# Layer 1's last modulation third moved into layer 0's choice, the sorts started before their vectors, and SP's loads reordered

## The chip, the cores and the metric
The kernel runs on one core of a Trainium2 chip. The metric is the device time of one execution in microseconds. A core has TensorE (PE, matrix products), VectorE (DVE), ScalarE (ACT), GpSimd (POOL) and SyncE (SP), which here only issues DMAs. Before the change the median of three runs was 3538.36 us (3538.24 to 3542.34).

## The reference
Two transformer layers work on 1024 tokens and 256 context tokens of width 1024, all in float32. Each layer has a modulation, a mixer (attention in layer 0; attention and a scan in layer 1) and a mixture of 16 experts.
```
def ada_modulation(cond, w_mod, b_mod):
    mod = jax.nn.silu(cond) @ w_mod + b_mod
    return jnp.split(mod[..., None, :], 6, axis=-1)      # sh1, sc1, gt1, sh2, sc2, gt2

def expert_choice_ffn(h, w_router, w_gate, w_up, w_down):
    aff = jax.nn.softmax(jnp.einsum('bnd,de->bne', h, w_router), axis=-1)
    gate, idx = lax.top_k(jnp.swapaxes(aff, 1, 2), cap)
    xg = h[bidx, idx]
    hid = jax.nn.silu(jnp.einsum('becd,edf->becf', xg, w_gate)) * jnp.einsum('becd,edf->becf', xg, w_up)
    out = jnp.einsum('becf,efd->becd', hid, w_down) * gate[..., None]
    return jnp.zeros_like(h).at[bidx, idx].add(out)
```
Layer 0 uses differential attention, a = p0 - lam * p1 of two softmax maps (the subtracted maps). Each expert takes its 128 best tokens (layer 0 also 32 context tokens).

## The kernel before
The kernel is one program of stages in order: modulation (first third), projection, differential attention, local attention, output mix with routing, experts of layer 0, then the front, scan, attention, mix and experts of layer 1. A stage has one written program for each engine, and semaphores between them. Weights are loaded by SP in the written order of its queue. Objects named "...Ahead" hold tiles of a following stage, and are loaded by the stage before it.

**Modulation.** The two 1024 x 6144 matrices are cut in six thirds of 2048 columns. `first` is multiplied in its own stage, `rest[0]` to `rest[4]` in the gaps of other stages by `RestOfModulation`. A third is eight steps: step n loads 128 rows (1 MB) into one of the slots, and `multiply` (matmuls at L312) makes four products of 128 x 2 by 128 x 512, in four strips of partitions of one PSUM bank. `add_bias` (L320) adds the bias in four VectorE instructions, `store` (L326) writes the third to DRAM. In the attention three thirds were done (`rest[0]`, `rest[1]` of layer 0 and `rest[4]`, the last of layer 1): 24 steps in pairs, after every second item, for items 0 to 23 of 40 (four heads of ten query tiles). The weights (`attn_a_mod_w`) are loaded from ACT's queue.

**The attention.** For each item TensorE makes scores (L1014) and turned weights (L1026), and multiplies the values (L1039). VectorE takes the scores out of PSUM (L939) and subtracts the maps (L960). GpSimd rotates the next head's queries and keys (L717 to L722) and normalises the output of a former head (L841 to L845).

**The choice.** `Choice.select` on VectorE sorts: 16 rounds of MAX8 (L2197), FIND_INDEX8 (L2198) and MATCH_REPLACE8 (L2200), each waiting for the one before, over the affinities of all experts. TensorE turns the result (L2235), VectorE makes indices, and GpSimd gathers the rows of expert 0 (`experts_xg` L2437, in layer 0 also `experts_xc` of the context, L2439). TensorE transposes them (L2639, L2642); VectorE and ACT scale them by `gain` and `shift` into `experts_xT`. Ahead of the sort VectorE waited for those vectors and made `gain` (L2569). In layer 0 TensorE meanwhile made the eight `opening` steps (`rest[2]`), whose first four weights the stage before had put in the tile of the down weights (`down_ahead_wd`), with PSUM bank `Y[1]`; and the four additions came after the first transposes. After the last expert comes `closing` (`rest[3]`).

**The experts.** For each expert TensorE makes 16 groups of eight products with the gate and up weights (L2684), the transposes of the next expert, and the products with the down weights (L2650, L2659). VectorE and ACT take the two halves of the result out of `Y[1]` and `Y[0]` (counters `yv` and `ya`), GpSimd adds the rows into DRAM. SP loads gate and up weights in two halves of 2 x 2 MB when TensorE has freed each, then 2 x 2 MB of down weights. Its order was: vectors, opening steps, gates and ups of expert 0, the store of the opening third with a wait, a wait for the first transposes, down weights of expert 0, `following.load` (layer 0: `FrontAhead`, 25 DMAs with two loads of 2 MB of `front_ahead_w`; layer 1: `FinishAhead`, ten DMAs), then the loop from expert 1 on.

## Time and profile before
| what | value |
|---|---|
| median of 3 runs | 3538.36 us (3538.24 to 3542.34) |
| the profiled execution's own time | 3540.56 us |
| its span | 3538.8 us |
| PE busy | 3262.9 us (92%) |
| DVE busy | 1251.9 us (35%) |
| ACT busy | 973.0 us (27%) |
| POOL busy | 494.0 us (14%) |
| HBM over the span | 192 GB/s |

The span runs from the first to the last record of the profiled execution. Times in rows are microseconds from its start. A line of a timeline is: start, duration, engine (PEld is the weight load of TensorE, "q" behind a name the engine's queue of instructions), line of the kernel, operation, output<-inputs, sizes, count, and in brackets how long the engine stood idle before it and what it waited for. One product of 32-bit numbers has two records. A line of the windows is: stretch, its length, busy time with count of PE, PEld, DVE, ACT and POOL, the granted TensorE clock as a share of full speed, the mean busy share of the DMA engines, and GB/s. A line of the DMA issues ends with the median time from issue to landing. L numbers are lines of the kernel before.

### The profile page before, as it was taken

What the parts mean: (1) busy time and instruction counts of PE and PEld (TensorE: products, weight loads), DVE (VectorE), ACT (ScalarE), POOL (GpSimd) and SP (SyncE); (2) the same over time, 40 slices, a digit from 0 to 9 for tenths busy, and PEclk for the clock granted to TensorE, in tenths of its full rate; (3) what the DMA queues carried; (4) which work ended last, traced back from release to release, by engine and by line L of the source; (5) the groups of instructions that cost most, each with busy time, mean ns of one, the idle gap of its engine ahead of it and who ended that gap; (6) DMA issues with size and microseconds to landing.
All of it is one profiled execution on the core that took longest, in us unless ns stands there. A gap on an engine that the chain in (4) does not pass through costs nothing. (4 is left out here: it accounts for less than half of the span.)

```text
span 3538.8 us, 53560 instructions
## 1 busy us (share of the span) xinstructions
PE 3262.9 (92%) x20520; PEld 2456.0 (69%) x20520; DVE 1251.9 (35%) x3001; ACT 973.0 (27%) x2247; POOL 494.0 (14%) x650
## 2 busy tenths in 40 slices
PE   6999989889993999999999989899799299999998
PEld 4888756667541878878778655566674188888886
DVE  3312178767655011011000153566675500101013
ACT  3211156756441011111110152235554111111111
POOL 0000234210010011111101130244101000000002
PEclk8999999989995999999999999999999699999999
DMA  6336454062355977777777640100314498888887
GB/s 222 125 104 113 117 193 166 15 159 80 117 200 183 332 248 268 256 246 263 257 253 265 218 170 0 54 21 30 99 38 161 142 365 317 316 316 313 313 313 267
DMA packets 377129, 675.77 MB, mean 191 GB/s; under 512 B 76232, under 2 KB 115016, under 8 KB 370752
## 3 DMA queue, kind: packets, MB, share of 16 engines
q1 hardware_dynamic: 343152, 561.60, 45.9%
q0 software_dynamic: 13616, 47.32, 5.5%
q10 hardware_dynamic: 20208, 64.87, 4.9%
q8 instruction: 88, 1.44, 0.2%
q14 instruction: 65, 0.53, 0.0%
HBM read 587.75 MB, written 92.20 MB: 192 GB/s over the span
## 5 line engine op out<-in xcount | busy, mean ns | idle before, releaser
L2684 PE MATMUL experts_gu_ps<-experts_xT,experts_wg 128*128 128x160 f32 (+1 forms) x4096 | 554.6, 289 | 12.7 <-DMA experts_wu<-in_l_w_up 7.0
L2684 PEld LDWEIGHTS experts_gu_ps<-experts_xT,experts_wg 128*128 128x128 f32 x4096 | 531.3, 193 | 28.0 <-issue 26.7
L2684 PE MATMUL experts_gu_ps<-experts_xT,experts_wu 128*128 128x160 f32 (+1 forms) x4096 | 550.1, 287 | 0.0
L2684 PEld LDWEIGHTS experts_gu_ps<-experts_xT,experts_wu 128*128 128x128 f32 x4096 | 525.7, 192 | 0.0
L2581 DVE TENSOR_TENSOR experts_hid<-experts_sil,experts_gu_ps 128x160 f32<-128x160 f32 (+1 forms) x256 | 77.8, 304 | 931.3 <-ACT experts_sil L2518 931.3
L2518 ACT ACTIVATE experts_sil<-experts_gu_ps 128x160 f32<-128x160 f32 (+1 forms) x256 | 74.3, 290 | 1110.8 <-PE experts_gu_ps L2684 1110.8
L2650 PE MATMUL experts_y_ps<-down_ahead_wd,experts_hid 128*128 128x512 f32 x512 | 228.3, 599 | 0.0
L2650 PE MATMUL experts_y_ps<-experts_wd,experts_hid 128*128 128x512 f32 x512 | 224.0, 595 | 1.2 <-DVE experts_hid L2581 1.2
L2650 PEld LDWEIGHTS experts_y_ps<-experts_wd,experts_hid 128*128 128x128 f32 x512 | 96.0, 190 | 118.1 <-issue 114.8
L2599 DVE TENSOR_SCALAR experts_y<-experts_y_ps,experts_wt 128x512 f32<-128x512 f32 x31 | 23.3, 750 | 436.9 <-PE experts_y_ps L2650 436.9
L2650 PEld LDWEIGHTS experts_y_ps<-down_ahead_wd,experts_hid 128*128 128x128 f32 x512 | 94.6, 190 | 114.4 <-issue 113.7
L2964 PE MATMUL front_pb_ps<-kept_hT,front_ahead_w 128*128 128x512 f32 (+1 forms) x384 | 138.7, 521 | 0.7 <-DVE kept_dt L3015 0.7
L2463 POOL DMA_INDIRECT moe<-experts_y,experts_ixs x31 | 49.4, 1594 | 575.4 <-DVE experts_y L2599 575.4
L3420 PE MATMUL scan_f_ps<-scan_w,kept_hT 128*128 128x512 f32 x256 | 117.1, 600 | 0.0
L2964 PEld LDWEIGHTS front_pb_ps<-kept_hT,front_ahead_w 128*128 128x128 f32 x384 | 72.4, 190 | 62.7 <-issue 59.4
L594 PE MATMUL proj_x_ps<-proj_ahead_w,proj_hT 128*128 128x256 f32 x480 | 115.1, 383 | 0.0
L594 PEld LDWEIGHTS proj_x_ps<-proj_ahead_w,proj_hT 128*128 128x128 f32 x480 | 92.0, 192 | 12.6
L2458 POOL DMA_INDIRECT moe<-experts_yc,experts_ixsc x16 | 25.7, 1609 | 530.7 <-ACT experts_yc L2535 530.7
L877 ACT ACTIVATE attn_a_e<-attn_a_e,attn_a_nmx 128x1280 f32<-128x1280 f32 (+1 forms) x80 | 96.6, 1209 | 9.9 <-DVE attn_a_e L939 9.9
L2504 ACT ACTIVATE experts_xT<-experts_tp_ps,experts_shift,experts_gain 128x128 f32<-128x128 f32 x132 | 49.6, 456 | 134.9 <-PE experts_tc_ps L2642 75.4
L1039 PE MATMUL attn_a_o_ps<-attn_a_v,attn_a_aT 128*128 128x128 f32 x672 | 83.1, 277 | 3.9 <-ACT attn_a_sq L892 3.9
L1039 PEld LDWEIGHTS attn_a_o_ps<-attn_a_v,attn_a_aT 128*128 128x128 f32 x672 | 78.3, 192 | 11.2 <-issue 7.5
(490 smaller groups left out, 4991.4 us busy)
## 6 DMA issues: line engine op xcount, KB each, us to landing
experts_wg<-in_l_w_gate SPq DMA_DIRECT2D x64, 2048.0 KB, 8.2
experts_wu<-in_l_w_up SPq DMA_DIRECT2D x64, 2048.0 KB, 13.1
down_ahead_wd<-in_l_w_down SPq DMA_DIRECT2D x32, 2048.0 KB, 14.9
experts_wd<-in_l_w_down SPq DMA_DIRECT2D x32, 2048.0 KB, 11.7
attn_a_mod_w<-in_l_w_mod ACTq DMA_DIRECT2D x20, 1024.0 KB, 6.4
proj<-proj_ob ACTq DMA_DIRECT2D x60, 256.0 KB, 2.3
proj_ahead_w<-in_l_w_in SPq DMA_DIRECT2D x6, 2048.0 KB, 9.5
mix_xr<-res SPq DMA_DIRECT2D x18, 512.0 KB, 3.6
```

The lines of the kernel that those rows point to most:

```text
L594: mm = nc.tensor.matmul(to[:, left], by[k], at[k], start=(k == 0 and n in (0, 1, 5)), stop=(k == HALF - 1 and n in (3, 5, 6)), skip_group_ ...
L877: nc.scalar.activation(e[:, s, m, 0:w], e[:, s, m, 0:w], ACT.Exp, bias=nmx[:, s, m:m + 1], scale=-1.0, accum_out=sums[:, s, m:m + 1]).then ...
L1039: mm = nc.tensor.matmul(O[:, 0:P], aT[:, kt, :], v[:, h % 2, kt, :], start=(kt * P == keys(t)[0]), stop=(kt == last))
L2458: pool.indirect_dma_start(moe.rearrange("t (j c) -> (t j) c", j=4), bass.IndirectOffsetOnAxis(ap=ixsc[:, 0:1], axis=0), yc[:], None, compu ...
L2463: pool.indirect_dma_start(moe, bass.IndirectOffsetOnAxis(ap=ixs[:, 0:1], axis=0), y[:], None, compute_op=ALU.add).then_inc(s_done, 16)
L2504: a = nc.scalar.activation(xT[:, k, 0:CAPX], TP[1][:, k - 4, :], ACT.Identity, bias=shift[:, 0, k:k + 1], scale=gain[:, 0, k:k + 1])
L2518: nc.scalar.activation(sil[:, f % 2, :], GU[f % 2][:, 0, 0:N], ACT.Silu).then_inc(sil_done, 1)
L2581: nc.vector.tensor_tensor(hid[:, f, :], sil[:, f % 2, :], GU[f % 2][:, 1, 0:N], ALU.mult).then_inc(hid_done, 1)
L2650: mm = nc.tensor.matmul(Y[h][:], hid[:, k, 0:CAPX], wd[:, h, k, :], start=(k == 0), stop=(k == KD - 1))
L2684: mm = nc.tensor.matmul(GU[f % 2][:, part, 0:N], w[:, h, k, c * P:(c + 1) * P], xT[:, k, :], start=(k == 0), stop=(k == KD - 1))
L2964: mm = nc.tensor.matmul(pb[n % 4][:, 0:width], w[:, s, k, at:at + P], hT[:, k, first:first + width], start=(k == 0), stop=(k == KD - 1))
L3420: mm = nc.tensor.matmul(F[:], kept.hT[:, k, t * P:(t + 1) * P], w[:, int(kind == "q"), k, :], start=(k == 0), stop=(k == KD - 1))
```

## The change
- `RestOfModulation` takes a list of PSUM banks `accs`, and third a uses bank a modulo their number. `store_third` stores one third and waits until it has landed.
- The attention multiplies two thirds (16 steps). The opening of layer 0's choice multiplies two, `rest[2]` and `rest[4]`, in `Y[1]` and `Y[0]`: 16 steps over the same four slots. The first third's additions are made inside the sort, after its eleventh round; the second's after the transposes. `ya` is counted up by one as `yv` is.
- In both layers the sort stands ahead of the wait for the vectors and of `gain`.
- SP's order: in layer 1 `following.load` comes ahead of the wait for the transposes; in layer 0 the two loads of `front_ahead_w` become `load_columns` and come after the gates and ups of expert 1 and the store of the second third.
```diff
+    def store_third(self, sp, a):
+        for j in range(GROUPS):
+            sp.wait_ge(self.added, START + GROUPS * a + j + 1)
+            sp.dma_start(self.rest[a][2][:, j * BANK:(j + 1) * BANK], self.rows[strip(j), a, :]).then_inc(self.stored, 16)
+        sp.wait_ge(self.stored, START + 16 * GROUPS * (a + 1))
...
-            opening = RestOfModulation(nc, st, K, [down.third], Y[1], "opening", down.places, down.w_in)
+            opening = RestOfModulation(nc, st, K, down.thirds, [Y[1], Y[0]], "opening", down.places, down.w_in)
...
                 link(nc.vector.match_replace(work[:], val[:, j:j + 8], work[:], -1.0))
+            if between and j == 80:
+                between()
...
                 load_gates_up(0)
                 if down:
+                    opening.store_third(sp, 0)
+                if ends:
+                    following.load(sp)
+                sp.wait_ge(tp_done, START + 1)
+                if down:
                     sp.wait_ge(opening.multiplied, START + opening.steps)
-                    opening.store(sp)
-                sp.wait_ge(tp_done, START + 1)
                 load_down(0)
-                following.load(sp)
-                with sp.Fori(0, E - 1) as e:
+                if not ends:
+                    following.load(sp)
+                load_gates_up(1)
+                if not ends:
+                    opening.store_third(sp, 1)
+                    following.load_columns(sp)
+                load_down(1)
+                with sp.Fori(1, E - 1) as e:
                     load_gates_up(e + 1)
                     load_down(e + 1)
...
                 choice.begin(dve, link)
+                choice.select(dve, link, first_third if down else None)
                 dve.wait_ge(vec_in, START + 16 * (2 * conds + 1))
                 for c in range(conds):
                     nc.vector.scalar_tensor_tensor(gain[:, c, :], gain[:, c, :], 1.0, g[:], ALU.add, ALU.mult).then_inc(vec_done, 1)
                 dve.wait_ge(vec_done, START + conds)
-                choice.select(dve, link)
                 transposed(0)
                 if down:
                     for j in range(GROUPS):
-                        opening.add_bias(dve, 0, j)
-                    dve.wait_ge(opening.added, START + GROUPS)
+                        opening.add_bias(dve, 1, j)
+                    dve.wait_ge(opening.added, START + GROUPS * 2)
                     dve.sem_inc(yv, 1)
+                    dve.sem_inc(ya, 1)
...
-                    pe.wait_ge((ya, yv)[h], START + e + (0, mods)[h])
+                    pe.wait_ge((ya, yv)[h], START + e + mods)
...
-                    differential_attention(nc, K, attn_ahead, near_ahead, projs[n], n, mixed, rest[:2] + rest[4:])
+                    differential_attention(nc, K, attn_ahead, near_ahead, projs[n], n, mixed, rest[:2])
...
-                down = over.enter_context(DownAhead(nc, K, rest[2])) if with_ctx else None
+                down = over.enter_context(DownAhead(nc, K, [rest[2], rest[4]])) if with_ctx else None
```

## Rows read from the trace of the kernel before
**Rows 1.** The page: the span of the profiled execution.
```profile
span 3538.8 us, 53560 instructions
```
**Rows 2.** Windows: head 2 of the attention (with four pairs), then head 3 (with none).
```profile
568.46:633.93 65.47, 62.56 (x441) 40.25 (x441) 55.93 (x141) 43.69 (x103) 28.28 (x17) 1.00 0.37 127
633.93:692.83 58.90, 55.51 (x376) 38.93 (x377) 48.03 (x134) 43.57 (x103) 13.78 (x10) 1.00 0.06 17
```
**Rows 3.** Timeline of TensorE, attention: start us, us, instructions, idle before and its releaser.
```profile
576.25 1.90 PE L312 MATMUL attn_a_m_ps<-attn_a_mod_w,cond_gate 128*2 128x512 f32 x16
578.08 0.70 PE L1014 MATMUL attn_a_s_ps<-attn_a_ahead_kT,attn_a_ahead_qT 64*128 64x256 f32 x4
...
588.56 0.70 PE L1014 MATMUL attn_a_s_ps<-attn_a_ahead_kT,attn_a_ahead_qT 64*128 64x256 f32 x4 [0.81 <-DVE attn_a_e L939]
```
**Rows 4.** Timeline of VectorE, the same stretch.
```profile
578.83 0.48 DVE L939 TENSOR_SCALAR_CACHE_REDUCE attn_a_e<-attn_a_s_ps,attn_a_nmx 128x256 f32<-128x256 f32 x1 [3.27 <-PE attn_a_s_ps L1014]
...
619.48 0.48 DVE L939 TENSOR_SCALAR_CACHE_REDUCE attn_a_e<-attn_a_s_ps,attn_a_nmx 128x256 f32<-128x256 f32 x1 [2.49 <-PE attn_a_s_ps L1014]
```
**Rows 5.** Timeline of the choice of layer 0, VectorE and TensorE.
```profile
1085.72 0.41 DVE L2192 MEMSET experts_strip<- 32x1 f32 x4 [0.34 <-PEq L1712]
1091.93 0.24 DVE L2569 SCALAR_TENSOR_TENSOR experts_gain<-experts_gain,experts_g 128x8 f32<-128x8 f32 x2 [5.80 <-DMA experts_g<-in_l_g_pre_ffn]
1092.21 0.69 DVE L2197 MAX8 experts_val<-listed_work 80x8 f32<-80x512 f32 x1
...
1095.19 1.04 PE L312 MATMUL experts_y_ps<-down_ahead_wd,cond_gate 128*2 128x512 f32 x8 [3.59 <-DMA down_ahead_wd<-in_l_w_mod]
...
1102.79 1.89 PE L312 MATMUL experts_y_ps<-down_ahead_wd,cond_gate 128*2 128x512 f32 x8 [0.63 <-DMA down_ahead_wd<-in_l_w_mod]
...
1129.64 0.40 PE L2235 MATMUL experts_tp_ps<-ident,experts_val 80*128 80x80 f32 x1 [24.96 <-DVEq L2208]
...
1138.86 1.94 PE L2639 MATMUL experts_tp_ps<-ident,experts_xg 128*128 128x128 f32 x8 [8.42 <-DMA experts_xc<-normed,experts_ixgc]
...
1143.89 2.83 DVE L320 TENSOR_TENSOR experts_opening_rows<-experts_y_ps,experts_opening_bias 2x512 f32<-2x512 f32 x4
```
**Rows 6.** Tile attn_a_mod_w: landing times of 24 step weights (1 MB each).
```profile
DMA to landing us min/median/max: 4.8/6.5/11.0
```
**Rows 7.** DMA issues of 1138:1146 (queues near empty), then of 1206:1216 (queues full).
```profile
experts_xc<-normed,experts_ixgc POOLq DMA_INDIRECT x1, 3.7
...
experts_xc<-normed,experts_ixgc POOLq DMA_INDIRECT x1, 6.6
```
**Rows 8.** Timeline of SP's queue from the choice of layer 0 to expert 1.
```profile
1148.09 1.02 SPq L2382 DMA_DIRECT2D down_ahead_wd<-in_l_w_down  x2
...
1180.91 1.38 SPq L2279 DMA_DIRECT2D front_ahead_w<-in_l_w_in  x2
```
**Rows 9.** Windows: TensorE clock and DMA, layer 0 (choice, then the start of expert 1).
```profile
1120.00:1124.00 4.00, 0.00 (x0) 0.00 (x0) 3.83 (x10) 0.00 (x0) 0.00 (x0) 0.50 0.92 340
...
1207.40:1212.00 4.60, 4.60 (x17) 4.60 (x18) 0.00 (x0) 0.00 (x0) 0.55 (x3) 0.50 1.04 308
```
**Rows 10.** Timeline of TensorE: the start of expert 1 of layer 0.
```profile
1207.36 4.61 PE L2684 MATMUL experts_gu_ps<-experts_xT,experts_wg 128*128 128x160 f32 x16 [7.04 <-DMA experts_wu<-in_l_w_up]
1214.44 2.34 PE L2684 MATMUL experts_gu_ps<-experts_xT,experts_wg 128*128 128x160 f32 x16
1216.62 2.34 PE L2684 MATMUL experts_gu_ps<-experts_xT,experts_wu 128*128 128x160 f32 x16
```
**Rows 11.** Timeline and one window of the choice of layer 1.
```profile
2776.53 0.37 SPq L2385 DMA_DIRECT2D experts_shift<-mod  x1
2780.33 0.69 DVE L2197 MAX8 experts_val<-listed_work 48x8 f32<-48x512 f32 x1
...
2802.00:2816.00 14.00, 0.00 (x0) 0.00 (x0) 13.38 (x31) 0.00 (x0) 0.00 (x0) 0.50 0.00 1
...
2820.15 1.12 POOL L2437 DMA_INDIRECT experts_xg<-normed,experts_ixg  x1 [0.88 <-DVEq L2229]
```

More of the change, by code:

```diff
@@ L281, with __init__ @@
     SLOTS = 4
-    def __init__(self, nc, st, K, rest, acc, name="mod", places=None, w_in=None):
-        self.nc, self.rest, self.acc, self.gate = nc, rest, acc, K.gate
+    def __init__(self, nc, st, K, rest, accs, name="mod", places=None, w_in=None):
+        self.nc, self.rest, self.accs, self.gate = nc, rest, accs, K.gate
         self.steps = KD * len(rest)
@@ L308, in multiply @@
         pe.wait_ge(self.w_in[n % self.slots], START + 16 * (n // self.slots + 1))
-        if k == 0 and a >= 1:
-            pe.wait_ge(self.added, START + GROUPS * a)
+        acc = self.accs[a % len(self.accs)]
+        if k == 0 and a >= len(self.accs):
+            pe.wait_ge(self.added, START + GROUPS * (a - len(self.accs) + 1))
         for j in range(GROUPS):
-            mm = self.nc.tensor.matmul(self.acc[strip(j), :], self.gate[:, :, k], self.places[n % self.slots][:, j * BANK:(j + 1) * BANK],
+            mm = self.nc.tensor.matmul(acc[strip(j), :], self.gate[:, :, k], self.places[n % self.slots][:, j * BANK:(j + 1) * BANK],
                                        start=(k == 0), stop=(k == KD - 1))
@@ L319, in add_bias, with __init__ @@
             dve.wait_ge(self.bias_in, START + 16 * GROUPS * len(self.rest))
-        self.nc.vector.tensor_tensor(self.rows[strip(j), a, :], self.acc[strip(j), :], self.bias[strip(j), a, :], ALU.add).then_inc(self.added, 1)
+        self.nc.vector.tensor_tensor(self.rows[strip(j), a, :], self.accs[a % len(self.accs)][strip(j), :], self.bias[strip(j), a, :], ALU.add).then_inc(self.added, 1)
+    def store_third(self, sp, a):
[3 more added lines that the diff above has]
+        sp.wait_ge(self.stored, START + 16 * GROUPS * (a + 1))
     def store(self, sp):
         for a in range(len(self.rest)):
-            for j in range(GROUPS):
-                sp.wait_ge(self.added, START + GROUPS * a + j + 1)
-                sp.dma_start(self.rest[a][2][:, j * BANK:(j + 1) * BANK], self.rows[strip(j), a, :]).then_inc(self.stored, 16)
-        sp.wait_ge(self.stored, START + 16 * GROUPS * len(self.rest))
+            self.store_third(sp, a)
 class DownAhead(Ahead):
-    def __init__(self, nc, K, third):
+    def __init__(self, nc, K, thirds):
         super().__init__(nc, K, "down_ahead")
-        self.third = third
+        self.thirds = thirds
         self.wd = self.sb("wd", [P, 2, KD, BANK])
@@ L341, in load @@
         for n, place in enumerate(self.places):
-            eng.dma_start(place, self.third[0][n * P:(n + 1) * P, :]).then_inc(self.w_in[n], 16)
+            eng.dma_start(place, self.thirds[0][0][n * P:(n + 1) * P, :]).then_inc(self.w_in[n], 16)
 def row(vec, width):
@@ L792, in differential_attention @@
         M = st.ps("m", [P, BANK])
-        later = RestOfModulation(nc, st, K, rest, M)
+        later = RestOfModulation(nc, st, K, rest, [M])
         rows = first.rows
@@ L2192, in begin, with select @@
             link(self.nc.vector.memset(self.strip[j * CAPC:(j + 1) * CAPC, :], float(j)))
-    def select(self, dve, link):
+    def select(self, dve, link, between=None):
         nc, work, val, idx, idf = self.nc, self.work, self.val, self.idx, self.idf
@@ L2277, in load, with load_columns @@
         sp.dma_start(self.cw[:, TAPS, :], columns(self.conv_b)).then_inc(self.cw_in, 16)
+    def load_columns(self, sp):
         for s in range(2):
@@ L2333, in experts @@
             gates_up = [w[:, h].rearrange("p k n -> p (k n)")[:, s * THIRD:(s + 1) * THIRD] for h in range(2) for w in (wg, wu) for s in range(2)]
[L2334 to L2335 removed]
+            opening = RestOfModulation(nc, st, K, down.thirds, [Y[1], Y[0]], "opening", down.places, down.w_in)
+            closing = RestOfModulation(nc, st, K, [last_third], [GU[0][:].rearrange("p a b -> p (a b)")], "closing", gates_up)
         if with_ctx:
@@ L2460, in scatter @@
                     pool.wait_ge(yv, START + e + mods + 1)
-                    pool.wait_ge(ya, START + e + 1)
+                    pool.wait_ge(ya, START + e + mods + 1)
                     pool.sem_inc(begun, 1)
@@ L2566, in _, with first_third @@
                 choice.begin(dve, link)
+                def first_third():
+                    for j in range(GROUPS):
+                        opening.add_bias(dve, 0, j)
+                choice.select(dve, link, first_third if down else None)
                 dve.wait_ge(vec_in, START + 16 * (2 * conds + 1))
```

1 line of the change is left out of this document (removed).

## The prediction
> **What bounds the kernel now.** I read the page first (span 3538.8 us [rows 1]; TensorE busy nearly throughout, so only places where TensorE waits or does avoidable work can pay), then the windows of the attention, then the timelines of the three stretches that the diff touches: the heads of layer 0's attention, the two choices (the sort of the affinities before the experts), and the start of the experts' loop. TensorE's own multiplications of the experts are not changed. So the whole effect must come out of these:
> - In the attention TensorE is nearly full: a head with four pairs of modulation steps takes 65.47 us with 62.56 us of TensorE, the next one without pairs 58.90 us with 55.51 us [rows 2].
> - In both choices VectorE's sort alone is the path. In layer 0 it starts at 1092.21, after a wait of 5.80 us for the small vectors; VectorE was free from 1086.13 (1085.72 + 0.41) [rows 5]. TensorE waits 24.96 us for the sort's end, and then 8.42 us for the gathered rows [rows 5]. In layer 1 the sort starts at 2780.33, and the stage at 2776.53 [rows 11].
> - At the start of expert 1 of layer 0 TensorE stands 7.04 us for the weights, and the first two groups after that run slowly [rows 10].
>
> **The attention: eight steps go.** The last third of layer 1's modulation was multiplied here in steps 16 to 23, as four pairs. A pair takes TensorE 1.83 us (576.25 to 578.08) [rows 3], four 7.3 us. Head 2 holds just these four and head 3 none: 65.47 - 58.90 = 6.57 us between them, 7.05 us in TensorE's busy time [rows 2]. Not all of it comes back, since VectorE is the other limit in head 2: it is busy 55.93 us there against 48.03 us [rows 2], for its operation with two operands in SBUF is slower beside GpSimd's rotations. After the first and the last pair VectorE waited 3.27 and 2.49 us for scores [rows 4], so these two pairs are worth their full 1.83. After the second pair TensorE already waited 0.81 us for VectorE [rows 3], so that pair only moves the wait and gives nothing; the third I count at 1.4. With a little for the four additions (2.83 us of VectorE as in [rows 5]) that go, the sum is 1.83 + 0 + 1.4 + 1.83 + 0.2 = 5.3 us. The bounds: 3.7 (two pairs alone) and 7.3 (all). The eight weight loads, four bias loads (scalar's queue) and four stores that go too lie beside other work: nothing.
>
> **The choice of layer 0.** Four pieces.
> - The sort no longer waits for the vectors: it starts at about 1086.17 instead of 1092.21, 6.04 us earlier. The two scalings go behind the sort, where VectorE waits for the gather anyway: 0.24 us, hidden. If that cover went it would cost just the 0.24.
> - In the middle of the sort, after 11 of 16 rounds, VectorE adds the biases of the first third: +2.83 us [rows 5], on the path. It waits for eight steps of TensorE, which ended at 1102.79 + 1.89 = 1104.7 [rows 5], and it is asked for at 1086.2 + 11 x 2.25 (36.07 us / 16 a round, 1092.21 to 1128.28) = 1111: no wait. The additions that stood behind the transposes remain, now for the second third. Net of both pieces: -3.2 us.
> - Eight more steps on TensorE, whose turn of the sorted maps is queued behind them. The steps before came at the pace of the loads: 1095.19 to 1102.79 is three loads, 2.53 us each [rows 5]. Eight more end at 1102.79 + 8 x 2.53 + 1.89 = 1124.9. The turn is due at 1129.64 - 3.2 = 1126.4. So it is 1.5 us clear and costs nothing; the cover is thin. The pace holds only while four slots keep the queue full. The shortest lone load took 4.8 us [rows 6]; with 1.9 us of slow multiplying and 0.6 us of issue that is 7.3 us a round trip against 4 x 2.53 = 10.1 us, so I take 2.53. Bound: the median 6.5 us [rows 6] gives 9.0, still under 10.1; from outside I allow 0 to +2 us.
> - Everything that SP loads behind them is late by 20 us. Expert 0's gate and up weights (8.4 MB) followed from 1102.8 and had landed at about 1124 [rows 5, 9], 396 GB/s; now they land at 1144. Their first half is there at 1134 and is used at 1144: no wait, the second half is used 17 us after the first. But the gather of expert 0's rows, 3.2 us earlier at 1130, now runs beside a full queue instead of an empty one. The smaller gather landed in 3.7 us beside near-empty queues and in 6.6 beside full ones [rows 7]: +2.9, and I take +2.8; bounds 0 and +4.
> The choice of layer 0 therefore gives -3.2 + 2.8 = -0.4 us, between -3.2 and +2.8.
>
> Beside this last piece stands a page of the Trainium skill, "DMA: Bandwidth & Descriptors", section "Queues, rings and completion order": each DMA engine takes turns between the queues that have work, a packet at a time. By that rule a gather of 0.5 MB would get half of the 396 GB/s and lose an estimated 1.3 us, not 2.8; the total would be 1.5 us lower than mine. The measured pair decides for me.
>
> **SP's new order, layer 0.** In the order in which SP issues: the gate and up loads of expert 0; four stores of the first third and a wait for them (they land behind the expert's weights, at about 1145 to 1146); the down weights, which went at 1148.09 [rows 8] and go no later now; 23 loads for the next stage, unchanged; then at once the gate and up weights of expert 1, where before two loads of 2 MB (front_ahead_w) went first, at 1180.91 [rows 8]. From there to TensorE's start at 1207.36 [rows 10] 26.5 us passed for about 8.4 MB; half of it is 13.2 us, so the first half of expert 1's weights lands at 1194. TensorE is ready at 1207.36 - 7.04 = 1200.3, or 1199.9 shifted. The wait of 7.04 us goes, with 5 us to spare. The slow stretch goes with it: the granted clock was 0.50 there [rows 9], that is the 1.2 GHz level, and two groups took 1214.44 - 1207.36 = 7.08 us instead of 2 x 2.18 [rows 10]: 2.7 us. Together -9.8 us. Bounds: 0 where the loads are not early enough, -9.8. What is late next: the four stores of the second third (2 us of SP), the 4.2 MB of front_ahead_w, and expert 1's down weights behind them. By 8.4 + 4.2 + 4.2 MB at 396 GB/s from 1181 they land by 1226; they are used after expert 1's sixteen groups of 2.18 us, at 1235. front_ahead_w itself is used in the next stage only. GpSimd's scatter now waits for the other half's counter with one more, and TensorE's first down multiplication for the additions; both are long done.
>
> **The choice of layer 1.** The sort starts with the stage: 2780.33 - 2776.53 = 3.8 us earlier [rows 11]; nothing is added in it. The ten loads of the last stage (5.2 MB) go before the wait for the transposes. The queues stood empty from 2802 [rows 11]; 5.2 MB at 396 GB/s ends at 2815.1, and the gather is issued at 2820.15 - 3.8 = 2816.3 [rows 11], just clear. Cost 0, bounds 0 and +1. Expert 1 of this layer has no wait that could go. So -3.8 us, bounds -3.8 and -2.8.
>
> **The sum.** -5.3 - 0.4 - 9.8 - 3.8 = -19.3 us. The profiled execution took 3540.56 us, 1.8 over its span [rows 1], and would come to 3521.3. The median of the runs, 3538.36, lies 2.2 below it, so the forecast is 3538.36 - 19.3 = 3519.1 us. All bounds at their best: -7.3 - 3.2 - 9.8 - 3.8 = -24.1, so 3514.3; at their worst without the stall kept: -3.7 + 2.8 + 2 - 9.8 - 2.8 = -11.5, so 3526.9.
>
> **Rivals.**
> - The stall at expert 1 stays, because SP's small loads or the stores before them take as long as they must and the loads of expert 1 come no earlier. For it: these small loads held SP to 1180.9, and the stores now land behind more. Against it: 4.2 MB fewer stand ahead. Only the rest counts: -9.5, 3528.9 us. Chance 8%.
> - VectorE bounds head 2 throughout, and the attention gives nothing: for it the 0.81 us [rows 3], against it the waits of [rows 4]. -14.0, 3524.4 us. Chance 8%.
> - The eight loads come slower, at 3.3 us each: TensorE's turn is late by 8 x 0.77 - 1.5 = 4.7 us. -14.6, 3523.8 us. Chance 14%.
> - The gather isn't slowed as much, by the turn-taking of queues as above: -1.5 more, 3517.6 us. Chance 6%.
> - The other side: the four slots do not overlap, and each of the eight loads costs a lone load's median 6.5 us [rows 6]. The last step ends at 1102.79 + 52 + 1.9 = 1156.7, the turn is 30.3 us late, and the expert's weights with it: -19.3 + 30.3 = +11.0, 3549.4 us. It decides from 2.53 + (1.5 + 19.3) / 8 = 5.1 us a load. Against it: the loads of [rows 5] came at 2.53 us. Chance 3%.
>
> **How the numbers follow.** The forecast has 61%. The range 3513 to 3530 takes in the bounds of the sum and the first four rivals. Measurements of this kernel tell a change from none at about 0.2%, 7.1 us. Faster by more: the forecast and the first four rivals, 97%, less 3% for two of them together (-14.6 + 9.8 = -4.8): 94%. Within: 3%. Slower: 3%.
>
> **What would show it.** Head 2 of the attention at about 60 us instead of 65.5; VectorE's first MAX8 right behind the memsets and the four additions behind the eleventh round without a wait; TensorE's last step ahead of the turn by 1 to 2 us; the first gather landing in 7 us; no wait of TensorE at expert 1, with the clock at 1.00; the sort of layer 1 starting with its stage. A wait over 2 us at the turn or at expert 1 makes the prediction wrong.

## The result and the profile after

The changed kernel takes 3521.55 us (median of 5 runs, 3519.24 to 3525.92); the kernel before, on the same chip, 3541.04 (5 runs, 3538.24 to 3542.74). The ratio is 0.995, with an interval of 0.9937 to 0.9964: 19.5 us faster, where 19.3 was forecast. The profiled execution took 3519.24 us:
```profile
span 3517.4 us, 53535 instructions
```
Against [rows 1] that is 21.4 us less. The two traces can be cut at the same instructions, the table adds up to that:

| stretch | before | after | change | forecast |
|---|---|---|---|---|
| up to the first transposes of the subtracted maps | 451.2 | 451.6 | +0.4 | 0 |
| attention, first to last of these transposes | 250.9 | 246.5 | -4.4 | -5.3 |
| to the choice of layer 0 | 383.6 | 383.1 | -0.5 | 0 |
| its start to TensorE's turn (its third product) | 44.3 | 40.9 | -3.4 | -3.2 |
| turn to the gathered rows' first transpose | 8.9 | 12.6 | +3.7 | +2.8 |
| to the first gate product | 5.5 | 5.6 | +0.1 | 0 |
| experts of layer 0, to the next front | 900.1 | 890.0 | -10.1 | -9.8 |
| front, scan, attention, mix of layer 1 | 732.0 | 728.1 | -3.9 | 0 |
| choice of layer 1, to its first down products | 84.3 | 80.8 | -3.5 | -3.8 |
| the rest | 678.0 | 678.2 | +0.2 | 0 |

The places that the change touches give -17.6 us (-4.4 + 0.4 - 10.1 - 3.5). Of the other 3.8, 3.5 lie in the scan of layer 1, which it doesn't touch (259.4 and 255.9 us). That is a matter of the execution: of the fourteen profiled in this study eight have 255.8 to 256.3 us there, among them two of kernels that are as before in most (the first two experiments), and six have 257.5 to 260.6. So the median of the runs is right to 0.2 us partly by luck; the working is to be held against -17.6.

**The attention.** Windows of heads 2 and 3 (columns as in [rows 2]):
```profile
570.61:629.90 59.29, 55.52 (x376) 38.92 (x377) 51.43 (x136) 43.62 (x103) 27.25 (x17) 1.00 0.16 46
629.90:688.70 58.80, 55.51 (x376) 38.89 (x376) 48.36 (x135) 43.51 (x103) 13.79 (x10) 1.00 0.06 17
```
Head 2 is 6.18 us shorter than in [rows 2] and almost as short as head 3; TensorE's busy time fell by the full 7.04 us. The timeline of TensorE at the place of the second pair, where [rows 3] had a wait of 0.81 us:
```profile
588.89 0.70 PE L1018 MATMUL attn_a_s_ps<-attn_a_ahead_kT,attn_a_ahead_qT 64*128 64x256 f32 x4 [2.65 <-DVE attn_a_e L943]
589.52 1.09 PE L1030 MATMUL attn_a_t_ps<-ident,attn_a_a 128*128 128x128 f32 x8
590.55 1.99 PE L1018 MATMUL attn_a_s_ps<-attn_a_ahead_kT,attn_a_ahead_qT 64*128 64x512 f32 x8
```
The pair's 1.83 us have become 1.84 us more of waiting (2.65 - 0.81), as the prediction said of this pair.

**The choice of layer 0.** Timeline of VectorE and TensorE:
```profile
1081.20 0.41 DVE L2196 MEMSET experts_strip<- 32x1 f32 x4 [0.34 <-PEq L1716]
1081.65 0.69 DVE L2201 MAX8 experts_val<-listed_work 80x8 f32<-80x512 f32 x1
...
1106.99 2.84 DVE L321 TENSOR_TENSOR experts_opening_rows<-experts_y_ps,experts_opening_bias 2x512 f32<-2x512 f32 x4
...
1110.00 1.89 PE L313 MATMUL experts_y_ps<-down_ahead_wd,cond_gate 128*2 128x512 f32 x8 [1.44 <-DMA down_ahead_wd<-in_l_w_mod]
1113.61 1.89 PE L313 MATMUL experts_y_ps<-down_ahead_wd,cond_gate 128*2 128x512 f32 x8 [1.72 <-DMA down_ahead_wd<-in_l_w_mod]
1116.10 1.89 PE L313 MATMUL experts_y_ps<-down_ahead_wd,cond_gate 128*2 128x512 f32 x8 [0.60 <-DMA down_ahead_wd<-in_l_w_mod]
1118.66 1.55 PE L313 MATMUL experts_y_ps<-down_ahead_wd,cond_gate 128*2 128x512 f32 x8 [0.67 <-DMA down_ahead_wd<-in_l_w_mod]
1121.95 0.29 PE L2241 MATMUL experts_tp_ps<-ident,experts_val 80*128 80x80 f32 x1 [1.74 <-DVEq L2214]
...
1134.70 1.94 PE L2662 MATMUL experts_tp_ps<-ident,experts_xg 128*128 128x128 f32 x8 [12.26 <-DMA experts_xc<-normed,experts_ixgc]
```
The sort starts behind the memsets, the four additions stand inside it without a wait, the steps come 2.5 us apart (with one of 3.6), and the last ends 1.74 us ahead of the turn. Then the gathered rows are waited for 12.26 us, where [rows 5] has 8.42. The tiles of the two gathers, experts_xg and then experts_xc, give the landing:
```profile
DMA to landing us min/median/max: 7.9/7.9/7.9
...
DMA to landing us min/median/max: 7.6/7.6/7.6
```
Before, the same two gathers had landed in 4.5 and 3.8 us.

**Expert 1 of layer 0.** TensorE's first groups and SP's queue:
```profile
1195.98 2.34 PE L2707 MATMUL experts_gu_ps<-experts_xT,experts_wg 128*128 128x160 f32 x16
...
1174.88 0.58 SPq L2383 DMA_DIRECT2D experts_wg<-in_l_w_gate  x1
...
1200.17 1.40 SPq L2287 DMA_DIRECT2D front_ahead_w<-in_l_w_in  x2
```
The wait of [rows 10] is gone and with it the slow groups: the window 1207 to 1212 has a clock of 1.00, the 2.4 GHz level, where [rows 9] had 0.50. The loads of expert 1 now go out at 1174.88, 21 us before they are used.

**The choice of layer 1.** VectorE's first MAX8 and TensorE's wait for the rows:
```profile
2758.43 0.69 DVE L2201 MAX8 experts_val<-listed_work 48x8 f32<-48x512 f32 x1 [0.32 <-PEq L1716]
...
2802.89 1.94 PE L2662 MATMUL experts_tp_ps<-ident,experts_xg 128*128 128x128 f32 x8 [7.09 <-DMA experts_xg<-normed,experts_ixg]
```
The stage starts at 2758.38 (SP), so the 3.8 us of [rows 11] are gone; the wait for the gather is the one that the trace of before had, 7.07 us.

### The profile page after: what moved, and what is told of

Same layout as the page of the kernel before. It is cut to its first block and busy times, and to the rows that moved or that the text cites. A ratio compares the mean times of both kernels' runs of the same rounds, so it can differ in the third digit from the quotient of the medians.

```text
span 3517.4 us, 53535 instructions
## 1 busy us (share of the span) xinstructions
PE 3264.6 (93%) x20520; PEld 2451.7 (70%) x20520; DVE 1249.3 (36%) x3001; ACT 973.8 (28%) x2247; POOL 493.2 (14%) x650
## 5 line engine op out<-in xcount | busy, mean ns | idle before, releaser
L598 PEld LDWEIGHTS proj_x_ps<-proj_ahead_w,proj_hT 128*128 128x128 f32 x480 | 91.9, 192 | 12.6
## 6 DMA issues: line engine op xcount, KB each, us to landing
proj<-proj_ob ACTq DMA_DIRECT2D x60, 256.0 KB, 2.3
```

Of the source, the lines that this page charges most:

```text
L598: mm = nc.tensor.matmul(to[:, left], by[k], at[k], start=(k == 0 and n in (0, 1, 5)), stop=(k == HALF - 1 and n in (3, 5, 6)), skip_group_ ...
```

## The experiments

The scan varies by up to 4.8 us from execution to execution, more than most of what is sought here, so each verdict below is read from stretches of one profiled execution, cut as in the table above (us):

| kernel | attention | choice 0 to turn | turn to transposes | experts 0 | scan | choice 1 | rest |
|---|---|---|---|---|---|---|---|
| before | 250.9 | 44.3 | 8.9 | 900.1 | 259.4 | 84.3 | 671.4 |
| after | 246.5 | 40.9 | 12.6 | 890.0 | 255.9 | 80.8 | 671.6 |
| after, once more | 245.7 | 40.9 | 12.6 | 890.0 | 255.8 | 80.8 | 672.1 |
| e1, sort first alone | 251.3 | 38.2 | 8.7 | 899.5 | 255.9 | 80.7 | 671.4 |
| e2, columns late alone | 251.1 | 44.1 | 8.8 | 890.2 | 256.0 | 84.3 | 671.3 |
| e3, third out of the attention | 247.2 | 43.8 | 8.8 | 902.1 | 257.9 | 84.1 | 671.8 |
| e4, third out of the choice | 246.6 | 38.2 | 9.0 | 892.0 | 257.5 | 80.8 | 671.7 |
| e5, four MB held | 246.9 | 41.1 | 8.7 | 892.3 | 260.4 | 80.7 | 671.5 |
| e6, additions late | 247.1 | 39.7 | 12.7 | 890.5 | 260.1 | 81.0 | 671.6 |
| e8, last stage's loads back | 247.1 | 40.9 | 12.6 | 890.2 | 255.8 | 79.2 | 671.6 |
| e9, columns ahead again | 247.3 | 40.9 | 12.5 | 897.6 | 255.8 | 79.4 | 671.4 |
| e10, one pair moved | 244.0 | 40.9 | 12.5 | 889.9 | 256.3 | 80.6 | 671.4 |
| e12, two MB held | 247.2 | 41.0 | 12.8 | 891.3 | 260.6 | 80.5 | 671.6 |
| e13, e12 + e6 + e10 | 243.9 | 39.2 | 12.7 | 890.5 | 255.9 | 80.5 | 671.2 |

"After, once more" is the changed kernel in the same rounds as e5, e6 and e10: 3518.79 us (4 runs, 3517.42 to 3519.81) against 3538.4, ratio 0.9941 (0.9925 to 0.9958).

**e1, the kernel before with the sort ahead of the vectors' wait, in both layers.**
```diff
+                choice.select(dve, link)
                 dve.wait_ge(vec_in, START + 16 * (2 * conds + 1))
...
-                choice.select(dve, link)
```


> The kernel before with one part of the change alone: in both choices the sort stands ahead of the wait for the vectors. My theory: the sort starts with the stage, 6.0 us earlier in layer 0 and 3.8 in layer 1, and both come through in full, since in layer 0 the gather (issued at 1127.5 instead of 1133.5) still runs beside empty queues. Total -9.8 us. A rival: the gather or the first group then waits for something else (the expert's weights, landed at 1124 and used at 1138), and less than 8 us come through.

3530.21 us against 3539.19, ratio 0.9976 (0.9966 to 0.9985). The way to the turn is 6.1 us shorter, the choice of layer 1 3.6, 9.7 together; the scalings behind the sort cost nothing that shows. Both pieces stand.

**e2, the kernel before with the two loads of front_ahead_w behind the gates and ups of expert 1.**
```diff
+    def load_columns(self, sp):
...
+                load_gates_up(1)
+                if not ends:
+                    following.load_columns(sp)
+                load_down(1)
-                with sp.Fori(0, E - 1) as e:
+                with sp.Fori(1, E - 1) as e:
```


> The kernel before with the loads of front_ahead_w put behind the gate and up loads of expert 1 of layer 0, and nothing else changed. My theory: the wait of 7.04 us at expert 1 goes, and the 2.7 us of slow clock after it: -9.8 us, with no other wait in its place. The rival (SP's many small loads hold expert 1's weights back in any case): a wait of over 2 us stays and the gain is under 6 us.

3529.24 us, ratio 0.9971 (0.9961 to 0.9982). The experts of layer 0 take 9.9 us less, and TensorE goes from expert 0's down products to expert 1 without a wait (timeline):
```profile
1195.54 7.13 PE L2656 MATMUL experts_y_ps<-down_ahead_wd,experts_hid 128*128 128x512 f32 x16
1202.51 2.34 PE L2690 MATMUL experts_gu_ps<-experts_xT,experts_wg 128*128 128x160 f32 x16
```
This edit alone is the whole of the stall.

**e3, the kernel before without the last third (it is multiplied nowhere).** ScalarE stores values of layer 1's other third in its place, four small stores more.
```diff
-                    differential_attention(nc, K, attn_ahead, near_ahead, projs[n], n, mixed, rest[:2] + rest[4:])
+                    differential_attention(nc, K, attn_ahead, near_ahead, projs[n], n, mixed, rest[:2])
```


> The kernel before with the last third of layer 1's modulation left out altogether (the attention makes 16 steps; in its place four small stores at the end of layer 0's experts put the third before it there a second time). My theory: head 2 of the attention goes from 65.5 to about 59.3 us (the changed kernel's trace shows -6.2), TensorE's wait for VectorE at the second pair grows from 0.8 to 2.7, and the total is -5.3 to -6.2 us. The rival (VectorE bounds the head): under 3 us. The other (TensorE alone bounds it): -7.3 us.

3536.29 us, ratio 0.999 (0.9981 to 1.0), 2.9 us under before where 5.3 to 6.2 were expected. The attention takes 3.7 us less than before. The experts of layer 0 take 2.0 us more: the next front's first transpose waits 19.7 us and not 17.6 (in e4 19.8), behind the four stores at the end that only e3 and e4 have. The attention's head 2 lasts 61.42 us, not the 59.29 of the changed kernel, though both execute the same there. TensorE's timeline behind the wait that the pair left shows why:
```profile
588.88 0.70 PE L1014 MATMUL attn_a_s_ps<-attn_a_ahead_kT,attn_a_ahead_qT 64*128 64x256 f32 x4 [2.65 <-DVE attn_a_e L939]
589.52 1.16 PE L1026 MATMUL attn_a_t_ps<-ident,attn_a_a 128*128 128x128 f32 x8
590.60 3.57 PE L1014 MATMUL attn_a_s_ps<-attn_a_ahead_kT,attn_a_ahead_qT 64*128 64x512 f32 x8
```
The eight score products take 3.57 us and not 1.99: they ran at the lower clock. The windows of the same 23 us, e3 and then the changed kernel, say it by the clock (before the last two columns):
```profile
588.88:612.00 23.12, 22.35 (x143) 15.25 (x144) 22.11 (x50) 15.04 (x32) 21.89 (x13) 0.93 0.04 13
...
588.88:612.00 23.12, 22.77 (x154) 15.75 (x154) 21.96 (x56) 16.89 (x38) 21.58 (x14) 1.00 0.05 13
```
Of the nine executions that have this wait of 2.64 to 2.65 us (the changed kernel twice, e3 to e6, e8, e9, e12) seven have a head 2 of 61.38 to 61.43 us; only the two of the changed kernel itself have 59.28 and 59.29. With the wait of 0.81 us (before, e1, e2) head 2 is 65.47 to 65.50, always. So the eight steps are worth 6.2 us in head 2 less 2.1 where the clock falls.

**e4, the changed kernel without the last third in the choice (it is multiplied nowhere); the sort first, the loads as changed.** The four small stores are those of e3, and the store of the second third goes.
```diff
-                choice.select(dve, link, first_third if down else None)
+                choice.select(dve, link)
...
-                down = over.enter_context(DownAhead(nc, K, [rest[2], rest[4]])) if with_ctx else None
+                down = over.enter_context(DownAhead(nc, K, [rest[2]])) if with_ctx else None
```


> The changed kernel with the last third left out of the choice of layer 0 (eight steps there instead of 16, four small stores at the end as in the run before). It measures what the moved third costs where it now is. My theory: the sort is 2.8 us shorter without the four additions, and the gather lands in 4.5/3.8 us instead of 7.9/7.6, as the queues are empty again, 3.5 us: total 6.3 us faster than the changed kernel, about 25 us faster than the kernel before. A rival: it is only the additions, 2.8 us, and the slow gather has another cause (the earlier sort).

3515.42 us, ratio 0.9933 (0.9917 to 0.995), 23.8 us under before where about 25 were expected; the four stores at the end cost 2.0 us in the experts here too. The way to the turn is 2.7 us shorter, from there to the transposes 3.6: 6.3 us. TensorE's timeline:
```profile
1118.17 0.40 PE L2241 MATMUL experts_tp_ps<-ident,experts_val 80*128 80x80 f32 x1 [19.77 <-DVEq L2214]
...
1127.46 1.94 PE L2664 MATMUL experts_tp_ps<-ident,experts_xg 128*128 128x128 f32 x8 [8.49 <-DMA experts_xc<-normed,experts_ixgc]
```
With the queues empty again the gathers land in 4.6 and 3.8 us and the wait is 8.49, as before the change. So the third costs in the choice 2.7 + 3.6 = 6.3 us, and gave 4.4 in the attention.

**e5, the changed kernel; SP holds the second half of expert 0's gates and ups (4 MB) until the first gather has landed.**
```diff
                     for h in range(2):
+                        if down and h == 1 and isinstance(e, int) and e == 0:
+                            sp.wait_ge(g_done, IX)
```


> The changed kernel, with SP holding back the second half of expert 0's gate and up weights (4.2 MB) until the first gather of layer 0 has landed. My theory: the slow gather (7.9/7.6 us instead of 4.5/3.8) comes from the full queues beside it. The first half of the weights lands at about 1129, the gather is issued at 1125.6 to 1127, so it is fast only in its second part: TensorE's wait before the transposes falls from 12.3 to 9.5 to 11 us, and the second half of the weights, landing at about 1144, is used at 1156, so no new wait: 1.5 to 2.8 us faster than the changed kernel. The rival (another cause): nothing, or 1 to 3 us slower by a wait for the second half.

3519.7 us against 3538.4, ratio 0.9941 (0.9925 to 0.9958). TensorE's waits behind the choice (us in total, times, longest):
```profile
PE experts_tp_ps L2664 <- DMA experts_xc<-normed,experts_ixgc: 8.2, 1, 8.2
...
PE experts_gu_ps L2709 <- DMA experts_wu<-in_l_w_up: 2.2, 1, 2.2
```
The gather's delay is gone in full, 3.9 us from turn to transposes, more than expected; with e4 that shows the weights in the queue as its cause. But the held weights came 2.2 us too late for the expert's second half, so 1.6 us remain.

**e6, the changed kernel with the first third's additions behind the first transposes of the sort.** SP's order changes with it: both thirds are stored behind the gates and ups of expert 1, and the loads of the next front's modulation vectors and of `front_ahead_w` come behind its down weights.
```diff
-                choice.select(dve, link, first_third if down else None)
+                choice.select(dve, link)
...
+                    for j in range(GROUPS):
+                        opening.add_bias(dve, 0, j)
                     for j in range(GROUPS):
                         opening.add_bias(dve, 1, j)
```


> The changed kernel with the first third's four additions out of the sort and behind the first transposes, next to the second third's; SP stores both thirds and loads the modulation's vectors for the next stage behind expert 1's gate and up loads. My theory: the sort ends 2.8 us earlier. But then TensorE's last of 16 steps, which now ends 1.7 us ahead of the turn, becomes the bound of the turn: only 1.5 to 1.9 us come through, and the rows show TensorE's turn directly behind its last step. The rival (the steps have room): the full 2.8 us. Against both: the eight additions delay the first product of expert 0, and the gain is smaller.

3523.88 us, ratio 0.9956 (0.994 to 0.9973). The timeline of TensorE:
```profile
1118.57 1.89 PE L313 MATMUL experts_y_ps<-down_ahead_wd,cond_gate 128*2 128x512 f32 x8 [0.68 <-DMA down_ahead_wd<-in_l_w_mod]
1120.39 0.40 PE L2241 MATMUL experts_tp_ps<-ident,experts_val 80*128 80x80 f32 x1
```
1.2 us of the 2.8 come back, less than the 1.5 to 1.9 expected; then the turn starts directly behind the last step, and the steps set it. That the steps are clear of the sort by little is so shown: the changed kernel has 1.74 us, and here the last step ended 0.4 us later from the stage's start (39.4 and 39.0 us). By the runs the kernel isn't faster: all four lie above the changed kernel's four of the same rounds (3522.16 to 3524.81), and the profiled one has the slow scan. So the gain is shown in its stage alone.

**e8, the changed kernel with the last stage's early loads back behind the down weights.**
```diff
-                if ends:
-                    following.load(sp)
                 sp.wait_ge(tp_done, START + 1)
...
-                if not ends:
-                    following.load(sp)
+                following.load(sp)
```


> The changed kernel with layer 1's early load of the output stage's operands back behind the down weights of expert 0, where the kernel before had it; all else as changed. Theory: the move cost and brought nothing, since the gathered rows of layer 1 are waited for by TensorE for 7.1 us in both kernels: the stage from the sort to the down projection and what follows stays within 0.3 us, 80.8 and 671.6 us. Rival (the load beside the gather delays it, as the full queue does in layer 0): layer 1's gather lands in 4.5 us or less here against 4.5 to 5 us in the changed kernel and the stage is 1 us or more shorter.

3524.38 us against 3540.88, ratio 0.9956 (0.994 to 0.9971). The choice of layer 1 is 1.6 us shorter, outside the 0.3 us that I had given. It isn't the gather, which is waited for 6.95 us here and 7.09 in the changed kernel. TensorE's timeline of e8, then of the changed kernel:
```profile
2808.03 3.38 PE L2704 MATMUL experts_gu_ps<-experts_xT,experts_wg 128*128 128x128 f32 x16 [1.95 <-ACT experts_xT L2518]
2811.25 1.95 PE L2704 MATMUL experts_gu_ps<-experts_xT,experts_wu 128*128 128x128 f32 x16
...
2806.79 3.76 PE L2707 MATMUL experts_gu_ps<-experts_xT,experts_wg 128*128 128x128 f32 x16 [1.95 <-ACT experts_xT L2521]
2810.34 3.11 PE L2707 MATMUL experts_gu_ps<-experts_xT,experts_wu 128*128 128x128 f32 x16
```
The clock rises one group earlier: 0.38 + 1.16 = 1.5 us. e9, in which these loads stand as in the changed kernel, has 79.4 us too, so it goes with the execution. The rival's gather doesn't show. e1, with the loads at their old place and the sort first, has 80.7 us against 80.8: the move neither costs nor gives.

**e9, the changed kernel with front_ahead_w back ahead of the gates and ups of expert 1 (one run).**
```diff
+                    following.load_columns(sp)
                 load_gates_up(1)
...
-                    following.load_columns(sp)
```


> The changed kernel with the columns of the next front (the loads of KB each in chunks of two or four bytes) back ahead of the first expert's successor's gates and ups on SP; all else as changed. Theory (the stall at expert 1 and its slow clock come from these columns standing ahead of the gates and ups): TensorE waits some 7 us at expert 1's first matmuls again and the stretch behind it runs at half clock, about 10 us more from the first gate matmul to the next front's first instruction (900 and not 890). Rival (the store of the second strips, or the third load of the front, shares the cause): the wait returns only in part, below 4 us.

3530.47 us. The experts of layer 0 take 7.6 us more; SP's queue and TensorE's timeline:
```profile
1178.43 1.20 SPq L2287 DMA_DIRECT2D front_ahead_w<-in_l_w_in  x2
...
1205.09 3.82 PE L2707 MATMUL experts_gu_ps<-experts_xT,experts_wg 128*128 128x160 f32 x16 [5.94 <-DMA experts_wu<-in_l_w_up]
1208.74 2.34 PE L2707 MATMUL experts_gu_ps<-experts_xT,experts_wu 128*128 128x160 f32 x16
```
The stall is back: 5.94 us of waiting and 1.5 (3.82 - 2.34) at the lower clock. It is 2 us less than I expected, in the wait (7.04 before) and in the slow stretch, whose length differs by execution. I had called these loads small columns; they are the two of 2 MB, and the expectation is wrong in that.

**e10, the changed kernel with one pair of the attention moved from item 15 to item 19, into the new wait of head 2.**
```diff
-                    strips = list(range(GROUPS)) if n % KD == 0 and 0 < n <= later.steps else []
+                    strips = list(range(GROUPS)) if n in (KD, 24) else []
...
-                    if n % 2 and n < later.steps:
-                        later.multiply(pe, n - 1)
-                        later.multiply(pe, n)
+                    if n % 2 and (n < later.steps - 2 or n == 19):
+                        step = n - 1 if n < later.steps - 2 else later.steps - 2
+                        later.multiply(pe, step)
+                        later.multiply(pe, step + 1)
```


> The changed kernel with one of the attention's eight pairs of modulation steps taken from its place after item 15 and put after item 19, where TensorE waits 2.65 us for VectorE since the change (0.8 before it), and its four additions after item 24. My theory: there TensorE's work is free, as VectorE bounds that stretch, and after item 15 it is on the path: -1.8 us in the attention, TensorE's wait back at 0.8 us, and no fall of the clock after it (in two of three runs without the pair the clock fell there, worth 2.1 us): head 2 at 59.3 us in every run. The rival (TensorE bounds the whole attention): no change, the pair costs its 1.83 us in either place.

3519.37 us, ratio 0.9945 (0.9928 to 0.9961). The attention takes 244.0 us, 1.7 to 2.5 under the changed kernel. e13 has the same edit and 243.9. The runs don't show it (the changed kernel had 3518.79 in the same rounds), and head 2 takes 59.7 us in both, not the 59.3 expected, so the pair isn't wholly free there. The moved pair fills the hole, the wait is 0.82 us again, and the clock stays up (timeline of e13):
```profile
585.32 1.90 PE L313 MATMUL attn_a_m_ps<-attn_a_mod_w,cond_gate 128*2 128x512 f32 x16
588.04 0.70 PE L1018 MATMUL attn_a_s_ps<-attn_a_ahead_kT,attn_a_ahead_qT 64*128 64x256 f32 x4 [0.82 <-DVE attn_a_e L943]
588.67 1.09 PE L1030 MATMUL attn_a_t_ps<-ident,attn_a_a 128*128 128x128 f32 x8
589.70 1.99 PE L1018 MATMUL attn_a_s_ps<-attn_a_ahead_kT,attn_a_ahead_qT 64*128 64x512 f32 x8
```

**e12, as e5, but only the last 2 MB are held (the wait stands between the second gates and the second ups).**
```diff
                         sp.dma_start(wg[:, h], half_of(w_gate, e, h)).then_inc(w_in["wg"][h], 16)
+                        if down and h == 1 and isinstance(e, int) and e == 0:
+                            sp.wait_ge(g_done, IX)
```


> The changed kernel with one more wait: SP issues the second half of expert 0's ups (the last 2 MB of the eight in the queue) only once the first gather has landed; the second half of the gates goes ahead of it as before. Holding both halves let TensorE start on the gathered rows 3.9 us earlier (8.7 us from the turn's first instruction to the gathered rows' first transpose, where the changed kernel has 12.6), but TensorE then waited 2.2 us for the second half's ups. Theory (both numbers are one budget: the bytes that are held come late by as much as they are held): with 2 MB held and not 4 the queue empties near the start of the gather, about 5 us later than with both held, so that part of the gain goes, 1.5 to 3.5 us remain, and the wait of 2.2 us is gone, since the ups land about 5 us earlier behind the gates. Net 1.5 to 3.5 us under the changed kernel in the stages from the turn to the next layer's front. Rival (the gather is slow until the queue is wholly empty): turn to first transpose stays above 11.5 us, net under 1 us. Rival: the ups are late all the same, with a wait of 2 us in the expert's matmuls, net 0.

3526.44 us, ratio 0.9952 (0.9937 to 0.9967). The first rival holds: 12.8 us from turn to transposes, nothing gained (and no wait for the ups). The windows of e12 (the last two columns are the DMA engines' share and GB/s), then of e5:
```profile
1130.91:1132.91 2.00, 0.00 (x0) 0.00 (x0) 0.00 (x0) 0.00 (x0) 0.98 (x5) 0.50 1.05 386
1132.91:1134.91 2.00, 0.00 (x0) 0.00 (x0) 0.00 (x0) 0.00 (x0) 0.00 (x0) 0.50 1.05 401
1134.91:1136.91 2.00, 0.00 (x0) 0.00 (x0) 0.00 (x0) 0.00 (x0) 0.00 (x0) 0.50 1.04 316
1136.91:1138.91 2.00, 0.91 (x5) 0.94 (x6) 0.00 (x0) 0.00 (x0) 0.36 (x2) 0.50 0.45 160
...
1129.39:1131.39 2.00, 0.00 (x0) 0.00 (x0) 0.42 (x3) 0.00 (x0) 1.70 (x2) 0.50 0.90 272
1131.39:1133.39 2.00, 0.00 (x0) 0.00 (x0) 0.00 (x0) 0.00 (x0) 0.96 (x5) 0.50 0.78 278
1133.39:1135.39 2.00, 0.99 (x5) 1.02 (x6) 0.00 (x0) 0.00 (x0) 0.36 (x2) 0.50 0.10 31
```
In e12 the gathers are issued at 1128.84 and 1130.24 and the engines stay near full until 1136.9; they land at 1136.8 and 1137.9 (7.9 and 7.6 us). In e5 the rate has already fallen to 272 GB/s in the window behind the first issue at 1129.31: the weights run out within 2 us of it, and the gathers land in 4.4 and 3.5. A queue that empties at the end of the gather helps nothing; my expectation took the gain as growing with the bytes held, and it doesn't.

The traces show where the time goes by the packets of the queues, q1 with SP's loads and q0 with the gathers (packets, MB, share). First the kernel before, 1133.55 to 1135.30 and 1135.30 to 1138.20, then the changed kernel, 1125.56 to 1129.96 and 1129.96 to 1133.50; each pair starts with the issue of the first gather:
```profile
DMA packets 0, 0.00 MB, mean 0 GB/s; under 512 B 0, under 2 KB 0, under 8 KB 0
...
q0 software_dynamic: 192, 0.66, 74.0%
...
q1 hardware_dynamic: 843, 1.69, 104.2%
...
q1 hardware_dynamic: 290, 0.59, 54.5%
q0 software_dynamic: 190, 0.65, 49.2%
```
The first packet of the gather comes 1.8 us behind its issue in the kernel before and in e1 to e5, and 4.5 us behind it in the changed kernel (twice), e6, e8, e9, e10, e12 and e13. So 2.7 us of the delay lie ahead of the first packet. Once the packets move, the two gathers have half of the bytes beside the weights and take 3.8 us and not 2.8. In e5 the weights have nearly run out when the first packet moves, at 1131.1. What holds the first packet back beside the full queue isn't shown.

**e13, the changed kernel with the edits of e12, e6 and e10 together.** The diff is these three.

> All that the runs point to, together: the changed kernel, with the second half of expert 0's ups held until the first gather has landed, the first third's additions behind VectorE's first transposes of the sort, and one pair of the last third's steps moved from item 15 to item 19 of the attention heads. Expected against the changed kernel: attention 1.7 to 2.5 us less (as the move alone measured), the way to TensorE's turn 1.2 us less (as the late additions alone measured), the gather 1.5 to 3.5 us less, less what the gather loses because it now starts 1.2 us earlier into the same queue (up to 1.2): sum 3.5 to 7, about 3514 us if the changed kernel is near 3519. Rival: the three are not additive, since all shorten the way to a queue that empties at a fixed time (it is filled by transfers of 12 plus 8 MB at 2.5 us a MB, issued from the stage's start): then the late additions bring nothing here and the sum is 3 to 4.5 us.

3518.67 us (3517.98 to 3523.03, 5 runs) against 3540.88, ratio 0.9942 (0.9928 to 0.9955). The attention is 243.9, the way to the turn 39.2 (1.7 less), the gather as slow as ever. That is 3.5 to 4.3 us in these places (2.6 or 1.8 + 1.7), and the expectation's lower end. It is in the rival's range of 3 to 4.5 too, but not by the rival's account: the late additions bring their part, and what is missing is the gather's. The interval overlaps that of the changed kernel, so the runs alone don't tell the two apart.

## Why the prediction was right, and where not

- **The attention, 5.3: mis-sized, 4.4.** In head 2 itself the four pairs gave 6.18 us, more than the 5.3: the third pair and the additions were worth more than counted. But heads 0 and 1, in which nothing was changed, together took 1.8 us longer in this execution (119.05 and 117.24 us), which varies: the attention of the nine executions with the wait of 2.65 us averages 246.8 us, that of the three with the old pairs 251.1, so 4.3. What the prediction missed is the clock: it said that the second pair "only moves the wait and gives nothing", and looked only at the wait's length. In seven of nine executions the longer wait is followed by slow products that take 2.1 us of head 2's gain. The two without them are the two of all fourteen whose heads 0 and 1 took longest (119.1 and 118.3 us, the others 116.1 to 117.8; the granted clock from 500 to 570 us was 0.95 in the first and 0.98 in e3). Over the whole attention the two kinds differ by just 1.0 us, 246.1 and 247.1.
- **The choice of layer 0, -0.4: +0.4.** Sort and additions as forecast, singly (e1: -6.1; e4: 2.7) and together. The eight steps cost nothing, clear by 1.74 us where 1.5 was forecast, with a pace of 2.5 us. The rival with loads of 3.3 us and the one with lone loads are out; the single step of 3.6 us is within the cover. The gather was the mis-sized term: +3.6 to +3.7 instead of +2.8. e4 and e5 show that the full queue is its cause. The pair of rows that I took it from compared another gather, of the context rows alone, at another place; the two at the place itself lost 3.4 (4.5 to 7.9) and 3.8 us (3.8 to 7.6). By the turn-taking of the Trainium skill's page "DMA: Bandwidth & Descriptors", section "Queues, rings and completion order", my estimate was 1.3 us. The trace agrees as far as the sharing goes: beside the weights the gathers' packets take 1.0 us longer. The other 2.7 us lie ahead of their first packet, and the estimate had no term for them.
- **The stall, -9.8: -10.1.** e2 alone gives 9.9 and e9 brings 7.6 back; the rival that it stays is out. What would be late next wasn't: TensorE has no wait for weights from expert 1 of layer 0 to the next front.
- **The choice of layer 1, -3.8: -3.5**, in e1 3.6.
- **Sum and median.** -17.6 in these places, -19.3 forecast; the errors are 0.9 in the attention and 0.8 (0.9 in the gather) in the choice. The rest of the measured difference lies in stretches that vary by the execution. The sum's worst case counts the +2 us of the steps twice, since the +2.8 of the choice (-3.2 + 4 + 2) holds it already; it should read -13.5 and 3524.9 us, which changes nothing above.

One thing the sum hid: the third's move does not pay by itself. It gives 4.3 us in the attention and costs 6.3 in the choice. e1 and e2 without it give 9.7 + 9.9 = 19.6 us in their places, 2 more than the 17.6 of the whole change. A kernel with just these two together wasn't run. By my estimate the move would come out 2 us ahead with e10's and e6's edits (-7.1 + 6.3 - 1.2; 7.1 = 251.1 - 244.0); the medians of the runs don't show that gain.

## What to carry to other kernels

Take each part of a change against its own alternative: a bundle's gain can hide a part that loses. When work is taken out of a busy TensorE stream where another engine is nearly as late, look at how long the hole is that it leaves, since the clock may fall behind it; spread the work that remains so that no hole opens. Before loads are queued ahead, ask what small, late transfer will run beside them: it pays for the full queue unless the large loads have nearly run out when its own first packets move (1.8 us behind the issue here), and holding back a part of them helps only if the rest is through by then.

## What the runs showed that I had not expected

- A wait of TensorE of 2.65 us, between products at 1.00 of the clock, was followed by products at the lower level in seven executions of nine, at a price of 2.1 us in head 2 (1.0 over the whole attention). A wait of 0.81 us at the same place never was, in three. The trace of before had such a spot in head 1: its timeline of TensorE has
```profile
516.08 3.45 PE L1014 MATMUL attn_a_s_ps<-attn_a_kT,attn_a_qT 64*128 64x512 f32 x8 [3.15 <-DVE attn_a_e L939]
```
  where these eight products take 1.99 us elsewhere; in all fourteen executions they take 2.56 to 3.79 at this place. It could have been read before the prediction.
- The landing of expert 0's first gather has two values here, 4.4 to 4.6 us and 7.9, and none between in fourteen executions; with 2 MB held (e12) it was 7.9 as with none. That is no rule for every gather: expert 1's first took 5.6 us in e12 and 7.2 in e6.
- The scan of layer 1, alike in all kernels, takes 255.8 to 260.6 us by the execution, and its executions fall in two groups (255.8 to 256.3 and 257.5 to 260.6). What decides that is open.
